# Another order at the boundaries: where the half sums stand among the matmuls, and what is prepared when

## What is computed

```python
# first block, both layers
u = rms_norm(h, norm_mix_pre[layer])
m = mixer(u) @ w_out                              # layer 0: "a_out"; layer 1: "b_out"
h = h + rms_norm(m, norm_mix_post[layer])         # boundaries a_post, b_post
f = swiglu_ffn(rms_norm(h, norm_ffn_pre[layer]), w_ffn_in[layer], w_ffn_out[layer])
h = h + rms_norm(f, norm_ffn_post[layer])         # boundaries a_fpost, b_fpost

def rms_norm(x, g):
    return x * lax.rsqrt(jnp.mean(x * x, axis=-1, keepdims=True) + RMS_EPS) * g
```

## Time and profile before

| | us |
|---|---|
| median of three runs | 2332.74 |
| lowest and highest run | 2332.67 and 2336.07 |
| profiled execution, its own time | 2332.67 |
| its span, first to last instruction | 2330.5 |
| PE busy | 2296.3 |
| DVE busy | 1324.2 |
| ACT busy | 882.1 |

### The profile page before, as it was taken

The page is one execution under the profiler, slowest core; times in us unless marked ns, Lnnn a source line. Parts: engine busy times, 40 slices in busy tenths (PEclk is TensorE's granted clock), DMA queues, the critical chain, the costliest instruction groups (busy, mean ns, idle before and its releaser), DMA issues.

```text
span 2330.5 us, 36325 instructions
## 1 busy us (share of the span) xinstructions
PE 2296.3 (99%) x14156; PEld 1945.9 (83%) x14156; DVE 1324.2 (57%) x1918; ACT 882.1 (38%) x1353; POOL 3.3 (0%) x5
## 2 busy tenths in 40 slices
PE   9999999999999999999999999999999999999998
PEld 7788888889987988888988877888888787888888
DVE  6564745532767755542567565766623895766532
ACT  6444422222525622222442354333322684333222
POOL 0000000000000000000000000000000000000000
PEclk9999999999999999999999999999999999999999
DMA  4222243323362233233242112323323203333332
GB/s 162 64 63 75 99 118 99 99 91 100 111 194 90 92 95 99 93 97 99 73 124 80 51 54 73 108 92 97 99 93 97 74 29 100 99 99 92 97 99 82
DMA packets 82603, 218.69 MB, mean 94 GB/s; under 512 B 10944, under 2 KB 31808, under 8 KB 82496
## 3 DMA queue, kind: packets, MB, share of 16 engines
q1 hardware_dynamic: 75600, 208.23, 28.5%
q10 hardware_dynamic: 6896, 8.92, 1.2%
HBM read 212.78 MB, written 4.34 MB: 93 GB/s over the span
## 4 chain that ended last, share of the span: by engine, by line
PE 88%; DVE 6%; ACT 3%; issue 1%; DMA 1%; SPq 0%; ACTq 0%; DVEq 0%
PE bank L465 25%; PE bank L467 24%; PE bank L466 24%; PE bank L686 3%; PE bank L685 3%; PE bank L687 3%; DVE w_lo L1694 1%; PE bank L844 1%; ACT w_hi L1146 1%; DMA raw<-weights_dram 1%; DVE acc L1723 1%; PE bank L1068 1%; PE bank L1054 0%; PE bank L957 0%; PE bank L512 0%
## 5 line engine op out<-in xcount | busy, mean ns | idle before, releaser
L1146 ACT ACTIVATE w_hi<-raw 128x1024 fp32r<-128x1024 f32 x378 | 400.1, 1060 | 1075.9 <-PE bank L467 933.3
L465 PE MATMUL bank<-u_hi,w_hi 128*128 128x512 f32 (+1 forms) x2090 | 794.8, 380 | 5.3 <-DVE w_lo L1694 3.3
L467 PE MATMUL bank<-u_hi,w_lo 128*128 128x512 f32 (+1 forms) x2090 | 786.7, 376 | 0.0
L466 PE MATMUL bank<-u_lo,w_hi 128*128 128x512 f32 (+1 forms) x2090 | 786.7, 376 | 0.0
L1694 DVE TENSOR_TENSOR w_lo<-raw,w_hi 128x1024 fp32r<-128x1024 f32 x378 | 461.4, 1222 | 399.8 <-ACT w_hi L1146 399.3
L465 PEld LDWEIGHTS bank<-u_hi,w_hi 128*128 128x128 f32 x2090 | 393.5, 188 | 82.9 <-DVE w_lo L1694 5.4
L467 PEld LDWEIGHTS bank<-u_hi,w_lo 128*128 128x128 f32 x2090 | 393.5, 188 | 72.1
L466 PEld LDWEIGHTS bank<-u_lo,w_hi 128*128 128x128 f32 x2090 | 393.8, 188 | 70.9 <-issue 1.2
L465 PE MATMUL bank<-hid_hi,w_hi 128*128 (+1 forms) x440 | 173.4, 394 | 0.0
L467 PE MATMUL bank<-hid_hi,w_lo 128*128 (+1 forms) x440 | 172.5, 392 | 0.0
L466 PE MATMUL bank<-hid_lo,w_hi 128*128 (+1 forms) x440 | 170.8, 388 | 0.0
(11 more groups left out here) (304 smaller groups left out, 2466.0 us busy)
## 6 DMA issues: line engine op xcount, KB each, us to landing
raw<-weights_dram SPq DMA_DIRECT2D x365, 512.0 KB, 3.5
bz<-gated_dram SPq DMA_DIRECT2D x32, 268.0 KB, 4.2
raw<-weights_dram ACTq DMA_DIRECT2D x13, 512.0 KB, 4.3
gated_dram<-bz SPq DMA_DIRECT2D x8, 274.0 KB, 3.1
h<-x_t_dram SPq DMA_DIRECT2D x8, 256.0 KB, 6.0
out_dram<-m SPq DMA_DIRECT2D x4, 256.0 KB, 2.4
out_dram<-m ACTq DMA_DIRECT2D x4, 256.0 KB, 2.5
cmask<-masks_dram ACTq DMA_DIRECT2D x4, 224.0 KB, 3.8
```

Of the source, the lines that this page charges most:

```text
L465: pe.matmul(out, wh, xh, start=start, stop=False)
L466: pe.matmul(out, wh, xl, start=False, stop=False)
L467: return pe.matmul(out, wl, xh, start=False, stop=stop)
L1146: act.activation(w_hi[:, j, :], raw[:, j, :], ACT.Copy).then_inc(hi_ready, 1)
```

## The change

Nothing is computed differently; the order changes in all three queues, and one call is added.

- PE: `post_sums(0)` moves from the first half-1 output chunk to the second (a_post, b_post: from product 5 to product 4 of the next; a_fpost, b_fpost: from the sixth pair of block and feature chunk to the third of the next). `post_sums(1)` moves from product 7 to product 4 of the half chunk of S + 1. The interleaving of S and S + 1 in half 1 is taken out. `mean_square` moves from behind the first product of the last half chunk to ahead of that chunk. At a_post and b_post `keep_awake(bank[0], 8)` is called ahead of the first input chunk.
- ACT: `high_part` of S, S + 1 and S + 2 come later among the `half_input` of half 0. At a_post and b_post the first kept pair of half 1 comes earlier, behind three of them; at a_fpost and b_fpost it comes behind all eight. The root of half 1 now stands ahead of `high_part(s + 3)`.
- DVE: in half 0 `low_part` of S stands behind the `u_lo` of step 3, that of S + 1 behind those of step 5. At a_post and b_post `add_pair(1, 0)` moves into step 2. `low_part` of S + 3 moves from ahead of the second `half_norm` to behind its step 1.

```diff
@@ -559,14 +559,14 @@
             def high_input(name):
                 return lambda: pe.wait_ge(uh_ready, SPLIT[name] + 1)
 
-            def half_chunk(s, half, out, xh, xl, ready=None, between=None, between_at=4):
+            def half_chunk(s, half, out, xh, xl, ready=None, between=None):
 
                 j = s % RING
                 pe.wait_ge(w_ready, s + 1)
                 for k in range(KC):
                     if ready:
                         ready(k)
-                    if between and k == between_at:
+                    if between and k == 4:
                         between()
                     last = product(out, weight(w_hi, j, k), weight(w_lo, j, k), xh[:, k, tokens(half)], xl[:, k, tokens(half)],
                                    k == 0, k == KC - 1)
@@ -593,27 +593,24 @@
                         last.then_inc(out_half, 1)
                 for n in range(4):
                     half_chunk(s + 4 + n, 1, half_bank(stat, 1, n // 2)[:, tokens(n % 2)], xh, xl,
-                               between=(lambda: post_sums(stat, 0)) if n == 0 else None, between_at=5).then_inc(slot_done, 1)
+                               between=(lambda: post_sums(stat, 0)) if n == 1 else None).then_inc(slot_done, 1)
 
             def halved_in(stat, s):
 
                 made, _, _, split = BOUNDARY[stat]
-                for n in range(4):
-                    pe.wait_ge(made_ready, MADE[made] + (4 + 2 * (n + 1) if "f" in stat else n + 1))
-                    half_chunk(s + n, 0, bank[n][:, tokens(0)], u_hi, u_lo,
-                               ready=(lambda k: pe.wait_ge(u_ready, SPLIT[split] + k + 1)) if n == 0 else None,
-                               between=(lambda: post_sums(stat, 1)) if n == 1 else None, between_at=7)
-                for k in range(KC):
-                    pe.wait_ge(u_ready, SPLIT[split] + KC + k + 1)
-                    for n in range(2):
-                        j = (s + n) % RING
-                        last = product(bank[n][:, tokens(1)], weight(w_hi, j, k), weight(w_lo, j, k),
-                                       u_hi[:, k, tokens(1)], u_lo[:, k, tokens(1)], k == 0, k == KC - 1)
-                        if k == KC - 1:
+                for half in range(2):
+                    for n in range(4):
+                        if half == 0:
+                            pe.wait_ge(made_ready, MADE[made] + (4 + 2 * (n + 1) if "f" in stat else n + 1))
+                            if n == 0 and "f" not in stat:
+                                keep_awake(bank[0], 8)
+                        last = half_chunk(s + n, half, bank[n][:, tokens(half)], u_hi, u_lo,
+                                          ready=(lambda k: pe.wait_ge(u_ready, SPLIT[split] + KC * half + k + 1)) if n == 0 else None,
+                                          between=(lambda: post_sums(stat, 1)) if half == 0 and n == 1 else None)
+                        if half:
                             last.then_inc(slot_done, 1)
-                half_chunk(s + 2, 1, bank[2][:, tokens(1)], u_hi, u_lo).then_inc(slot_done, 1)
-                half_chunk(s + 3, 1, bank[3][:, tokens(1)], u_hi, u_lo, between=lambda: mean_square(split), between_at=1)\
-                    .then_inc(slot_done, 1)
+                            if n == 2:
+                                mean_square(split)
 
             def out_chunks(part, xh, xl, free, ready, ready_hi=None):
 
@@ -695,13 +692,13 @@
                                 last = half_product(*into_half(n, half, c, kk))
                     last.then_inc(slot_done, 1)
 
-                def back_halved(n, half, between=None, between_at=(1, 0)):
+                def back_halved(n, half, between=None):
 
                     pe.wait_ge(w_ready, s1 + HALF + n + 1)
                     for c in range(4):
+                        if between and c == 1:
+                            between()
                         for kk in range(2):
-                            if between and (c, kk) == between_at:
-                                between()
                             last = half_product(*into_half(n, half, c, kk))
                         if n == HALF - 1 and (c == 1 or c == 3 and half == 0):
                             last.then_inc(out_half, 1)
@@ -724,7 +721,7 @@
                         for n in range(HALF - 4, HALF):
                             back_halved(n, 0)
                         for n in range(HALF - 4, HALF):
-                            back_halved(n, 1, (lambda: post_sums(f"{l}_fpost", 0)) if n == HALF - 4 else None, (2, 1))
+                            back_halved(n, 1, (lambda: post_sums(f"{l}_fpost", 0)) if n == HALF - 3 else None)
                         continue
                     back(half, 0, first=True)
                     with pe.Fori(0, 2) as i:
@@ -1245,21 +1242,23 @@
                     act.wait_ge(out_half, OUT_HALF[made] + pair + 1)
                     keep_pair(stat, 0, pair)
                 half_root(stat, 0)
-                half_input(stat, 0, range(4))
+                half_input(stat, 0, range(3))
+                if "f" not in stat:
+                    act.wait_ge(slot_done, s - 2)
+                    keep_pair(stat, 1, 0)
+                half_input(stat, 0, range(3, 5))
                 high_part(s)
-                half_input(stat, 0, range(4, 6))
+                half_input(stat, 0, range(5, 7))
                 high_part(s + 1)
+                half_input(stat, 0, range(7, 8))
                 if "f" in stat:
                     act.wait_ge(out_half, OUT_HALF[made] + 3)
-                else:
-                    act.wait_ge(slot_done, s - 2)
-                keep_pair(stat, 1, 0)
-                half_input(stat, 0, range(6, 8))
-                high_part(s + 2)
+                    keep_pair(stat, 1, 0)
                 act.wait_ge(slot_done, s)
                 keep_pair(stat, 1, 1)
+                high_part(s + 2)
+                half_root(stat, 1)
                 high_part(s + 3)
-                half_root(stat, 1)
                 half_input(stat, 1, range(KC))
                 for c in range(KC):
                     square(split, c, h[:, c, :])
@@ -1737,7 +1736,7 @@
                     dve.wait_ge(acc_ready, n if pair + i else ACC[stat] + 3)
                     dve.tensor_tensor(acc[:, t], acc[:, t], sq[:, pair, tokens(i)], ALU.add).then_inc(acc_ready, 1)
 
-            def half_norm(stat, half, low_before):
+            def half_norm(stat, half, low_after):
 
                 made, _, _, split = BOUNDARY[stat]
                 t = tokens(half)
@@ -1753,25 +1752,27 @@
                         x, y = (z[:, 2 * p:2 * p + 2, t] for z in (m, h))
                         dve.wait_ge(normed, NORMED[made] + PAIRS * half + p + 1)
                         dve.tensor_tensor(y, y, x, ALU.add).then_inc(h_ready, 1)
-                    if step in low_before:
-                        low_part(low_before[step])
                     if step >= 2:
                         for c in (2 * step - 4, 2 * step - 3):
                             dve.wait_ge(uh_ready, SPLIT[split] + KC * half + c + 1)
                             dve.scalar_tensor_tensor(out=u_lo[:, c, t], in0=h[:, c, t], scalar=pre_gain(split, c),
                                                      in1=u_hi[:, c, t].bitcast(F32), op0=ALU.mult, op1=ALU.subtract)\
                                .then_inc(u_ready, 1)
+                    if step in low_after:
+                        low_part(low_after[step])
+                    if step == 2 and half == 0 and "f" not in stat:
+                        add_pair(stat, 1, 0)
 
             def boundary(stat, s):
 
                 for pair in range(2):
                     add_pair(stat, 0, pair)
-                half_norm(stat, 0, {3: s, 4: s + 1})
-                add_pair(stat, 1, 0)
+                half_norm(stat, 0, {3: s, 5: s + 1})
+                if "f" in stat:
+                    add_pair(stat, 1, 0)
+                add_pair(stat, 1, 1)
                 low_part(s + 2)
-                add_pair(stat, 1, 1)
-                low_part(s + 3)
-                half_norm(stat, 1, {})
+                half_norm(stat, 1, {1: s + 3})
                 sum_squares(BOUNDARY[stat][3])
                 low_over(s + 1)
 
```

## The result

| | before | after |
|---|---|---|
| median of 5 runs each, us | 2332.74 (2332.53 to 2336.07) | 2346.61 (2345.96 to 2348.14) |
| ratio, 95% interval | | 1.0062 [1.0051, 1.0073] |
| span of the profiled execution, us | 2330.5 | 2345.8 |

The kernel became slower by 13.9 us, 0.62%.

What follows compares the result with a forecast made beforehand. One DVE and ACT chain, on which PE waits, was taken to set each boundary's end. Twice 4.5 us (a_post, b_post) plus twice 2.9 (a_fpost, b_fpost) made 14.8, giving 2347.5 us, 0.6% slower; range 2340.5 to 2352.

Steps and rivals of the forecast that it cites:

- 1, first sum: First sum moves 7 products, 2.48 us, at a_post and b_post; 5 products, 1.77 us, at the FFN boundaries.
- 3, start of S: First input slot waits for its late `w_lo`: PE starts it 3.1 us late at a_post, 1.26 at a_fpost.
- 5, wait for `u_lo` 7: Before the second input slot, PE waits 0.5 us for the last `u_lo`, then 0.8 more for `w_lo`.
- 6, second sum: Second sum's earlier place gives 1.06 us back, but after a late start; first `m` of half 1 3.3 late at a_post.
- 7, `mean_square`: Fourth slot's `w_lo` inside the second norm adds 1.14 us; `mean_square` of a_post moves from 255.83 to 260.3.
- 8, wait at L550: PE still waits 0.4 us at `mean_square`; no wait would mean PE, not the chain, sets the end.
- 9, wait at the sixth slot: Stall at 265.73 moves by the same 4.5 us as the chain; PE waits 0.35 less of its 0.72.
- Step 4: `keep_awake` at a_post and b_post costs nothing, hidden in the first slot's wait; uncovered, 1.8 us each, 3.6 in all.
- Step 8: Dropping half 1's interleaving costs nothing: PE waits 0.6 us for `u_lo`, but the DVE and ACT chain ends last.
- Nobody waits for these: In the second pass, the first two slots come free earlier and their loads start earlier, with nothing waiting for them.
- 2.9 stays: Behind each FFN boundary, what follows waits on the same root, so the 2.9 us delay remains.
- rival of the clock: PE idling at FFN boundaries halves the clock, 1.7 us per fall: 2351 with two, 2354 with four; chance 0.15.

Runs made afterwards that it cites:

- e6: Kernel after with only the first sum, `post_sums(0)`, put back to its old place: 5.9 us over the kernel before, ratio 1.0027.
- e1: Kernel after with all of PE's order put back, ACT and DVE keeping the new order: 11.1 us over the kernel before, ratio 1.0052.
- e7: Kernel after with the fourth input slot (S+3) prepared ahead of the root and second norm, as before: 11.1 us over the kernel before, ratio 1.0043.
- e3: Kernel after without its `keep_awake` calls: 15.1 us over the kernel before, ratio 1.0072.
- e10: Kernel after without its `keep_awake` calls, run a second time: 15.1 us over the kernel before, ratio 1.0069.
- e4: Kernel before with the two `keep_awake` calls added ahead of the first input chunk of a_post and b_post: 3.5 us over the kernel before, ratio 1.0016.
- e8: Kernel after with the first two input slots of half 1 interleaved again: 14.0 us over the kernel before, ratio 1.0057.
- e2: Kernel before with PE's new order, ACT and DVE keeping the old order: 6.6 us over the kernel before, ratio 1.0024.
- e5: Kernel before with only the first sum, `post_sums(0)`, moved to its new place: 6.1 us over the kernel before, ratio 1.0026.
- e12: Kernel before with the sixth slot's low part made earlier in layers a and b, and the second sum one product earlier: -2.1 us, ratio 0.9990.
- e11: Kernel before with the sixth slot's low part made ahead of the first gate product in layers a and b: -1.2 us, ratio 0.9991.

## Why the prediction was right

By its own steps, on the clock of before:

| step | predicted | measured |
|---|---|---|
| 1, first sum; a_fpost | 226.50; moved 1.77 | 226.50; moved 1.77 |
| 3, start of S, a_post; a_fpost | 237.25; 603.63 | 237.15; 603.61 |
| 5, wait for `u_lo` 7; for `w_lo` S+1 | 0.5; 0.8 | 0.24; 0.61 |
| 5, start of S+1 | 241.41 | 241.39 |
| 6, second sum; first `m` of half 1 | 242.83; 244.53 | 242.89; 244.48 |
| 7, `mean_square` | 260.3 | 260.24 |
| 8, wait at L550 | 0.4 | 0.3 by the starts |
| 8, wait for `u_lo` of half 1 | 0.6 | 0.35 |
| 9, wait at the sixth slot | 0.72 less 0.35 | 0.48 |
| to `mean_square`, four boundaries | 4.5, 2.9, 4.5, 2.9 | 4.4, 3.0, 4.4, 3.0 |
| PE behind the boundary | the same | 4.5, 2.7, 4.4, 2.9 |

- The starts of steps 1 to 7 held to 0.1 us in the profile, and the causes behind them in the runs: the moved sum is 7.8 of the chain (e6), the queues cost time with PE untouched (e1). Step 7 held at the FFN boundaries too: `m` of half 1 came 1.8 us late for 1.7, and the `w_lo` of S+3 added its 1.14. (That e7 gives back only 0.7 there is the price of the other place, ahead of the norm.)
- Step 4, `keep_awake` hidden: shown by e3 and e10 (no gain from removing it). The price if uncovered, 3.6, was 3.5 in e4.
- Step 8, dropping the interleaving costs nothing: shown by e8. The prediction also wanted L550 to wait 0.4 still; the profile after lists no wait there. By its own words this would have meant that PE sets the end, but the starts show it held for 0.3 us until the last add ends, and in e8, where PE is freed of the `u_lo` waits, a wait of 0.83 comes back with no time gained. The chain still sets the end.
- Steps 8 and 9 were wrong in two small things. "Nobody waits for these" (the earlier loads) fails at a_fpost. There the `w_lo` of the sixth slot stood idle for its load before; in the kernel after it no longer does, and the gate work behind it, with PE's wait of 0.34 at 627.94, comes 7.26 us later where `mean_square` comes 7.84. The timelines of DVE in the kernel before and, below the dots, in the kernel after:

```profile
624.54 1.23 DVE L1694 TENSOR_TENSOR w_lo<-raw,w_hi 128x1024 fp32r<-128x1024 f32 x1 [0.63 <-ACT w_hi L1146]
...
631.81 1.23 DVE L1693 TENSOR_TENSOR w_lo<-raw,w_hi 128x1024 fp32r<-128x1024 f32 x1
```

  In e8, interleaved again, the idle time is back (0.71 us) and PE leaves a_fpost 3.05 us late, for 2.73 in the kernel after. So the interleaving itself had a price of 0.3 us there, by way of the load. And "2.9 stays" behind the FFN boundaries fails by 0.2 at a_fpost, while at b_fpost it holds.
- The waits inside the boundaries were predicted 0.1 to 0.3 us too long while the starts were right. The idle time that the profile lists begins at the modelled end of the last matmul, which lies behind the pace (each row here is 0.28 us long at a pace of 0.12); a distance between starts is what to compute with.
- The rival of the clock did not come. Its counter-argument was misread: 2.56 us idle of 5.4 is 0.53 busy, which is nearer to the 0.36 of the row with the fall than to the 0.80 of the other; the clock stayed up all the same. Windows of the kernel after (stretch, busy us of PE, PEld, DVE, ACT, POOL, then PE's granted clock) show it at 1.00 behind a wait of 1.2 us at both kinds of boundary:

```profile
238.00:242.00 4.00, 3.29 (x24) 2.89 (x24) 3.26 (x7) 3.52 (x7) 0.00 (x0) 1.00 0.00 0
609.00:613.00 4.00, 3.17 (x25) 2.79 (x24) 3.23 (x7) 4.00 (x9) 0.00 (x0) 1.00 0.27 111
```

  The Trainium skill (TensorE: Matmul & The Clock Gate, "A second HAM failure mode: psum-queue depth-cycling") describes a kernel whose clock swings because TensorE idles for very short times between groups of matmuls. The short waits at these boundaries didn't do it.
- The sum was 14.8 predicted and 14.8 on the chain, of which PE keeps 14.4, while the medians give 13.9 and 14.0 and the profiled spans 15.3. The rest lies outside the boundaries, where executions differ by a microsecond and more: all 25 runs of the kernel after have a median of 2348.10, and the medians of the kernel before lie between 2332.74 and 2333.96. So that the forecast was met to 0.9 us is in part luck; the shift at the four boundaries is not.

## What to carry to other kernels

When one chain over slower engines sets the end of a stage, ask of each edit only how much later the chain's first link starts and what is put between its links; the busiest engine's waits move about without changing the end. Parts of a change on such a chain don't add: measure each one done alone and each one undone (here 6.1 and 8.0 us for the same line). An early consumer, such as the second sum, is worth something only once its input is early too. And compare single profiles stage by stage, each against a start just ahead of it, since the stretches between can differ by more than the effect.

## What the runs showed of the hardware

**Behind an idle gap of 3 us the clock fell in three of four cases, behind gaps of 1.2 to 1.5 us at the same places in none.** Without `keep_awake` PE idles 3.03 us at a_post and 3.27 us at b_post. Behind this the granted clock fell to half in both places in e3, and at a_post only in e10. Windows of e3_no_awake:

```profile
238.00:241.00 3.00, 3.00 (x16) 3.00 (x15) 2.26 (x6) 2.84 (x6) 0.00 (x0) 0.50 0.00 0
794.00:797.50 3.50, 3.50 (x19) 3.50 (x19) 2.76 (x6) 3.17 (x7) 0.00 (x0) 0.52 0.00 0
```

Windows of e10_no_awake_again, the same code:

```profile
238.00:241.00 3.00, 3.00 (x20) 3.00 (x19) 2.27 (x5) 3.00 (x7) 0.00 (x0) 0.63 0.00 0
...
794.00:797.50 3.50, 2.67 (x21) 2.30 (x20) 2.76 (x6) 3.50 (x8) 0.00 (x0) 1.00 0.00 0
```

At half the clock, the 1.2 GHz level, the matmuls stand 0.21 us apart instead of 0.12 (timeline of PE in e3_no_awake):

```profile
237.62 0.42 PE L465 MATMUL bank<-u_hi,w_hi 128*128 128x256 f32 x1 [3.03 <-issue]
237.84 0.42 PE L466 MATMUL bank<-u_lo,w_hi 128*128 128x256 f32 x1
238.05 0.42 PE L467 MATMUL bank<-u_hi,w_lo 128*128 128x256 f32 x1
```

A fall cost the chain only 0.2 to 0.3 us (a_post 4.6 and 4.7, for 4.4), since the slow chunk took the place of the waits for `u_lo` 7 and `w_lo` of S+1.

**At two places away from the boundaries a fall cost 1.0 to 1.4 us, and it came in some profiles only.** In the kernel before it falls at 1342, and so it does at the same work in the kernel after. In e2, e3, e4, e5 and e12 it stayed up there, and PE gains 1.3 to 1.4 us on the kernel before. At 725 to 729 it fell in e2, e5, e6 and e11, and PE loses 1.0 us on it there. Neither place is part of the change. The prediction had priced a fall at 1.7. Windows of e5_sum0_late, clock up at the first place, and, below the dots, of e2_pe_new, clock down at the second:

```profile
1349.00:1353.00 4.00, 3.91 (x78) 3.35 (x79) 4.00 (x8) 1.16 (x2) 0.00 (x0) 1.00 0.03 9
...
728.50:731.90 3.40, 3.09 (x60) 3.12 (x64) 3.17 (x5) 0.63 (x1) 0.00 (x0) 0.50 0.03 7
```

**A weight load lands late now and then.** The weight loads issued from 228 to 235 us, that of slot S+1 at a_post among them, took 3.9 us at most in the kernel before, and up to 5.1 us in e11 and e12, whose loads there are the same. The issues of weights in e12_sixth_sum1 from 228 to 235 us, with the times from issue to landing:

```profile
DMA to landing us min/median/max: 3.5/3.6/5.1
```

and what became of it on ACT and on PE, by their timelines:

```profile
234.03 1.06 ACT L1146 ACTIVATE w_hi<-raw 128x1024 fp32r<-128x1024 f32 x1 [2.17 <-DMA raw<-weights_dram]
```

```profile
236.80 0.38 PE L465 MATMUL bank<-u_hi,w_hi 128*128 128x256 f32 x1 [1.01 <-DVE u_lo L1761]
```

`w_hi` stands ahead of `u_hi` in ACT's queue, so the late load delays the chain: `mean_square` of a_post comes 1.1 to 1.3 us later in those two profiles. The runs of e12 reach from 2328.92 to 2334.35, and such landings are a likely share of it; that they make up all of it was not shown.
